# Nine more 512-column chunks of a two-block layer as seven block products, with a weight ring of three slots

## The reference, cut to what matters

```python
h = rms_norm(x, g_norm);  proj = h @ w_in             # q_a k_a v_a q_i ... q_m z_m gate_logits
branch = einsum('nbsw,nwd->nbsd', ys, w_branch)
merged = einsum('bsnd,nbsd->bsd', sigmoid(gate_logits), branch)
x = x + merged @ w_out                                 # wout0, wout1
...
h = _rmsnorm(x, norm_mix);  h @ w_in_2                 # dq dk (diff. attention), gv gg gqk gr (GLA), dv
kv = _rmsnorm(mem_2, norm_mem) @ w_ckv                 # ckv0 .. ckv3
```

## Time and profile before

| | before |
|---|---|
| median of the 3 runs (lowest, highest) | 1147.48 us (1147.24, 1147.68) |
| the profiled execution: its time, its span | 1148.03 us, 1146.3 us |
| PE busy | 943.7 us, 82% |
| DVE, ACT, POOL busy | 341.6, 175.3, 102.6 us |
| DMA, share of 16 engines over the span | 63.9%, 253 GB/s |
| mean granted clock of PE | 0.925 of full speed (2.4 GHz) |

### The profile page before, as it was taken

How to read it: one execution, slowest core, us unless ns; L and a number is a source line. 1 busy time by engine, 2 the same in 40 slices (tenths; PEclk the granted TensorE clock), 3 DMA queues, 4 the chain that set the end, 5 groups by cost and what they waited for, 6 DMA issues and landing times.

```text
span 1146.3 us, 11508 instructions
## 1 busy us (share of the span) xinstructions
PE 943.7 (82%) x4732; PEld 531.3 (46%) x4732; DVE 341.6 (30%) x879; ACT 175.3 (15%) x380; POOL 102.6 (9%) x121
## 2 busy tenths in 40 slices
PE   7999999899999999999999999565655566565736
PEld 3555485679999464455544555221221212131312
DVE  3217933764232221535545424010000101010101
ACT  2114232431000012212312211000000000000000
POOL 2013110145443010100000000000000000000000
PEclk9999999999999999999999999887787878697979
DMA  9546232224445264432209458999999999999996
GB/s 327 177 154 219 85 137 74 74 75 147 148 148 185 75 220 146 147 144 77 74 1 342 177 219 340 430 428 427 428 429 428 428 428 427 428 427 428 429 420 240
DMA packets 64020, 290.33 MB, mean 253 GB/s; under 512 B 8983, under 2 KB 11870, under 8 KB 52190
## 3 DMA queue, kind: packets, MB, share of 16 engines
q1 hardware_dynamic: 63966, 289.57, 63.9%
HBM read 288.51 MB, written 1.05 MB: 253 GB/s over the span
## 4 chain that ended last, share of the span: by engine, by line
PE 62%; DMA 28%; DVE 5%; SPq 2%; ACT 2%; issue 1%; ACTq 0%; DVEq 0%
PE ACC L500 24%; PE ACC L515 8%; PE AUX L1033 7%; PE ACC L643 6%; DMA ring<-in_w_e_down_dram 5%; DMA ring<-in_w_e_gate_dram 5%; PE ACC L539 4%; PE AUX L1063 3%; DMA BIG<-in_w_e_up_dram 3%; DMA PJ<-in_w_e_up_dram 3%; DMA SQE<-in_w_e_up_dram 3%; DMA PJ<-in_w_e_down_dram 3%; DMA BIG<-in_w_e_gate_dram 2%; PE ACC L925 2%; DMA SQE<-in_w_e_gate_dram 2%; PE AUX L550 2%
## 5 line engine op out<-in xcount | busy, mean ns | idle before, releaser
L1033 PE MATMUL AUX<-ring,R 128*32 128x512 f32 x416 | 115.4, 718 | 53.6 <-DMA BIG<-in_w_e_up_dram 20.2
L500 PE MATMUL ACC<-ring,BIG 128*128 128x512 f32 (+2 forms) x384 | 159.1, 573 | 0.2 <-ACT BIG L1513 0.2
L500 PE MATMUL ACC<-ring,R 128*128 128x512 f32 (+1 forms) x296 | 129.2, 590 | 2.8 <-DVE R L1677 2.1
L500 PEld LDWEIGHTS ACC<-ring,BIG 128*128 128x128 f32 x384 | 72.5, 190 | 81.6 <-issue 73.6
L515 PE MATMUL ACC<-BIG,ring 128*128 128x256 f32 (+1 forms) x464 | 107.3, 385 | 0.0
L515 PEld LDWEIGHTS ACC<-BIG,ring 128*128 128x128 f32 (+1 forms) x464 | 85.2, 188 | 16.1 <-issue 4.1
L500 PEld LDWEIGHTS ACC<-ring,R 128*128 128x128 f32 x296 | 55.8, 192 | 65.4 <-issue 64.2
L1033 PE MATMUL AUX<-R 128*32 128x512 f32 x112 | 62.7, 723 | 24.7 <-DMA ring<-in_w_e_gate_dram 14.6
L1033 PE MATMUL AUX<-BIG,R 128*32 128x512 f32 x192 | 55.6, 745 | 29.0 <-DMA PJ<-in_w_e_up_dram 22.3
L2187 DVE SCALAR_TENSOR_TENSOR R<-R,AUX 128x512 f32<-128x512 f32 x8 | 5.5, 687 | 235.9 <-ACT R L1608 235.9
L1033 PEld LDWEIGHTS AUX<-ring,R 128*32 128x32 f32 x416 | 28.3, 129 | 93.4 <-issue 93.4
(11 more groups left out here) (311 smaller groups left out, 1287.6 us busy)
## 6 DMA issues: line engine op xcount, KB each, us to landing
ring<-in_w_in_dram SPq DMA_DIRECT2D x20, 2048.0 KB, 7.9
ring<-in_w_e_gate_dram SPq DMA_DIRECT2D x14, 2048.0 KB, 27.2
ring<-in_w_e_up_dram SPq DMA_DIRECT2D x12, 2048.0 KB, 30.8
ring<-in_w_e_down_dram SPq DMA_DIRECT2D x10, 2048.0 KB, 30.1
PJ<-in_w_e_down_dram SPq DMA_DIRECT2D x8, 2048.0 KB, 31.7
BIG<-in_w_e_up_dram SPq DMA_DIRECT2D x8, 2048.0 KB, 32.4
PJ<-in_w_e_gate_dram SPq DMA_DIRECT2D x6, 2048.0 KB, 27.3
BIG<-in_w_e_down_dram SPq DMA_DIRECT2D x6, 2048.0 KB, 26.4
```

The lines of the kernel that those rows point to most:

```text
L500: mm = nc.tensor.matmul(bank[:, t * 512:t * 512 + width], lhs[:, i, t * P:(t + 1) * P], w[:, i, a:a + width], start=(i == 0), stop=(i == k ...
L1033: mm = nc.tensor.matmul(bank[r, :], M_xt[:, k, r], w[e][:, k, :], start=(k == 0), stop=(k == KD - 1))
```

## The change

Besides the six gates, nine chunks become seven block products: qm, wout0, wout1, ckv0, dq, dk, gv, ckv1 and gg. They take a second form of `project_blocks`: rows stationary, weights moving, 28 matmuls of 256 columns. The gates keep their own form (`turned=True`). The fourth slot of the ring is set aside: it holds S_a, S_b (first half) and T_x (second half), and the ring has three slots until ckv2; wo1 and wco1 are then loaded into the fourth. ckv3 is loaded before wo0. The fourth weight sum is now written over w12, may start after m1 and m2, and S_b no longer waits for the whole chunk before. POOL makes weight sums for all 15 chunks; the row sums for merged, mem_2 and x1 are made by DVE (`row_sums`, four instructions each). DVE sums the products of each chunk (`combine`, eight instructions), and so it, not ACT, frees the PSUM banks of these chunks. ckv0 and ckv1 are scaled by ACT afterwards in SBUF, gg's tanh is read from SBUF, and the sum into x is made from a temporary (`TMP`).

```diff
-        T_x = R2[:, :].rearrange("p (i k q) -> p i k q", i=4, k=4)
+        block_chunks = ["qm"] + gate_chunks + ["wout0", "wout1", "ckv0", "dq", "dk", "gv", "ckv1", "gg"]
+        WS = slots[RING - 1]
+        S_a, S_b = (WS[:, 1024 * i:1024 + 1024 * i].rearrange("p (k n) -> p k n", k=4) for i in range(2))
+        T_x, T_mem2 = (t.rearrange("p (i k q) -> p i k q", i=4, k=4) for t in (WS[:, 2048:4096], R5[:, 2048:4096]))
...
+        c = chunk_at["ckv2"]
+        slot_no = [i % (RING - 1) for i in range(c + 3)] + [RING - 1] + [i % (RING - 1) for i in range(c, c + 3)] + [RING - 1]
...
+            def project_blocks(name, src, T, sums, base=0, after=None, turned=False):
+                w11, w12, w21, w22 = (w[:, 4 * j:4 * j + 4, 256 * i:256 * i + 256] for i in range(2) for j in range(2))
+                x = quarters(src)
+                products = [(w11, x[0][0], 0, 0), (w12, x[1][0], 0, 0), (S_a, T[:, 0], 1, 1), (S_b, T[:, 1], 3, 2),
+                            (w21, T[:, 2], 0, 3), (w22, T[:, 3], 0, 4), (w12, x[1][1], 4, 0)]
...
+                                mm = nc.tensor.matmul(bank, right[:, k, :], left[:, k, :], start=(k == 0), stop=(k == 3))
...
-            project("wout0", R1T, ready=merged_half)
-            project("wout1", R1T)
+            pe.wait_ge(merged_ready, 1)
+            project_blocks("wout0", R1T, T_x, merged_sums, after=lambda done: pe.wait_ge(merged_ready, 2) if done == 4 else None)
+            project_blocks("wout1", R1T, T_x, merged_sums)
...
-            project("dq", XT3)
-            project("dk", XT3)
-            project("gv", XT3)
-            project("ckv1", R2T)
+            project_blocks("dq", XT3, T_x, x1_sums)
+            project_blocks("dk", XT3, T_x, x1_sums)
+            project_blocks("gv", XT3, T_x, x1_sums)
+            project_blocks("ckv1", R2T, T_mem2, mem2_sums)
...
+            def weight_sums(name):
...
                 if c:
                     pool.wait_ge(block_products, 3 * c - 1)
                 add(S_a, w21, w22, ALU.add, w_sums, 4 * c + 1)
                 add(w21, w11, w21, ALU.subtract, w_sums, 4 * c + 2)
-                if c:
-                    wait_full(pool, (gate_chunks[c - 1], "high"))
                 add(S_b, S_a, w11, ALU.subtract, w_sums, 4 * c + 3)
-                pool.wait_ge(block_products, 3 * c + 2)
-                add(S_b, w12, S_b, ALU.subtract, w_sums, 4 * c + 4)
...
+                pool.wait_ge(block_products, 3 * c + 1)
+                add(w12, w12, S_b, ALU.subtract, w_sums, 4 * c + 4)
...
+            row_sums(T_x, quarters(kt(R1[:, :], KD)), merged_sums)
             drain_rows("mem2", R2T, GC_MEM2)
+            wait_drained(dve, ("mem2", 1, 1))
+            row_sums(T_mem2, quarters(R2T), mem2_sums)
             dve.wait_ge(rows_squared, 4)
             rsqrt(2, SMALL[:, 64:66], SMALL[:, 78:80]).then_inc(mem2_scaled, 1)
...
+            for h in range(2):
+                combine(f"wout{h}", by_rows(TMP))
+                part = X3[:, :, h * 512:(h + 1) * 512]
+                v.scalar_tensor_tensor(out=part, in0=TMP, scalar=0.25, in1=part, op0=ALU.mult, op1=ALU.add).then_inc(x_added, 1)
...
+            combine("dq", by_rows(DQ))
             dve.wait_ge(decay_e, 1)
...
+            combine("dk", by_rows(DK))
+
+            def apply_d():
+                combine("gv", by_rows(GV), range(2))
+                scale_heads(hv(DQ[:, 0, :], 8), 0, 8)
+                scale_heads(hv(DK[:, 0, :], 8), 16, 8)
+                combine("gv", by_rows(GV), range(2, 4))
```

More of the change, by code:

```diff
@@ L638, in project_blocks @@
                     bank = (low if m < 4 else high)[:, 256 * (m % 4):256 * (m % 4) + 256]
[L639 to L645 removed]
+                    if w_sum:
+                        pe.wait_ge(w_sums, 4 * c + w_sum)
+                    if x_sum:
+                        pe.wait_ge(sums, base + x_sum)
+                    for j in range(2 if turned else 1):
+                        for k in range(4):
+                            if turned:
+                                mm = nc.tensor.matmul(bank[:, j * P:(j + 1) * P], left[:, k, j * P:(j + 1) * P], right[:, k, :],
+                                                      start=(k == 0), stop=(k == 3))
+                            else:
+                                mm = nc.tensor.matmul(bank, right[:, k, :], left[:, k, :], start=(k == 0), stop=(k == 3))
+                            n += 1
+                            last = k == 3 and (j == 1 or not turned)
+                            if m == 6 and last:
                                 mm.then_inc(high_full, 1)
[L647 removed]
+                            elif m in (1, 3, 5) and last:
                                 mm.then_inc(block_products, 1)
@@ L774, in end_m @@
                     attend("M", 4 + (done - 6) // 12, 5 + (done - 6) // 12)
-            project_blocks("gate00", start_m)
-            project_blocks("gate01", end_m)
+            project_blocks("gate00", XT3, T_x, x0_sums, after=start_m, turned=True)
+            project_blocks("gate01", XT3, T_x, x0_sums, after=end_m, turned=True)
             wait_drained(pe, ("O", first_unit["A"] + 7))
@@ L1317, in _ @@
             g.tensor_tensor(KE, kt(GK, 2), kt(EE, 2), ALU.mult).then_inc(gla_products, 1)
+            for name in ("gv", "ckv1", "gg"):
+                weight_sums(name)
             for t in range(TT):
@@ L1507, in drain_mem2, with scale_mem2 @@
                 last.then_inc(free_sem(key), 1)
-            drain_mem2("ckv0", R1v, 0)
+            def scale_mem2(key, T3, c):
+                wait_drained(act, key)
+                for t in range(TT):
+                    part = T3[:, t, c:c + 512]
+                    last = a_.activation(part, part, ACT.Copy, scale=SMALL[:, 78 + t:79 + t])
+                link(last)
+            scale_mem2("ckv0", R1v, 0)
             drain("gr", [(GRT[:, :], lambda b: b[0:16, 0:S])])
```

231 lines of the change are left out of this document (118 added, 113 removed).

## The result

The changed kernel takes 1154.78 us (median of 4 runs, 1154.24 to 1155.85) against 1147.36 us for the kernel before, measured beside it (4 runs, 1147.14 to 1147.68): ratio 1.007, 95% interval 1.0057 to 1.0083. It is slower, as was forecast: by 7.4 us, where the forecast had 4.6. The profiled execution took 1154.90 us, its span is 1153.1; the one before took 1148.03, span 1146.3.

A forecast was written before the change was run, and what follows sets the result against it. PE was taken to bound the kernel up to about 700 us, the expert weights' DMA stream from 716 us. Costs of 23.4 us less 18.8 saved gave +4.6 on 1147.48, so 1152.1 us, own range 1148 to 1156, overall range 1134 to 1157.

The forecast's parts named there:

- A chunk of 12.1 us, 1.66 saved: Each of nine chunks on PE, as 56 instructions of 256 columns, takes 12.1 us; 14.9 us saved for nine.
- Around qm, 3.0 of at most 4.2 us: At qm, earlier sums and no ACT drain remove PE's waits of 1.17, 1.59 and 1.00 us; 3.0 us saved, bounds 0 to 4.2.
- Three waits: 7.3, 6.8 and 7.8 us: Before wout1, dk and ckv1, PE waits this long for the low bank, as POOL's sums hold DVE's two-SBUF-input instructions.
- the second rival's case: Before dk, POOL does not hold the decay chain's scans: wait 3.3 us, not 6.8; 1148.6 us; chance 0.18, shared with one wait halved or absent.
- gr 0.8, gv's fourth product 0.7: Smaller PE waits: gr 0.8 us for ckv0's bank, gv's fourth product 0.7 us for S_b.
- The ring of three, nothing: Weight loads with three slots: 7.9 us to land, wanted 19 us after issue, 11 us of slack, so no cost.
- The wait of 0.86 us at wcq1: PE's wait at 611 us for wcq1 goes, since its slot is free earlier; 0.86 us saved.
- One for one to the end: What PE gains or loses before the cross attention ends moves the whole expert-weight stream equally; expert gates start about 4.6 us later.
- the first rival: Waits on POOL do not bind: cost 1.5 + 0.7 us, saving 18.8, giving 1130.9 us; waits mostly absent had chance 0.24.
- The ring starves nobody: Judges the rival that loads taking 19 us instead of 7.9 make PE wait: 1153 to 1160 us, chance 0.04.
- The change reaches the end: Judges the rival that the expert stream hides the change: 1147.5 us, chance 0.04.

The follow-up runs named there:

- pe_fill_half: Changed kernel plus useless matrix products on PE behind wout0 (17), dq (15) and gv (17), to keep it busy through the three waits: 1149.90 us.
- order_three: Changed kernel with DVE's work reordered at three places and POOL's at one, around the combines of wout0, dq, gv and dk; nothing left out: 1144.86 us.
- no_pool_sums: Changed kernel with POOL's first three weight sums for wout1, dk, gv and ckv1 replaced by tiny memsets, so those chunks use stale sums: 1129.01 us.
- order_five: order_four with gg and the turn of KE ahead of the turned heads on PE, and the QLZ copies behind the norm chain: 1137.72 us.
- order_four: order_three with mem_2's rsqrt behind both wout combines, combine(gv) split between the padded copies, combine(ckv1) inside and around the norm chain: 1143.07 us.

## Why the prediction came out as it did

**The direction was right, and so was the mechanism of the waits; what the clock adds behind a wait was missing.** That the time still fell between 1148 and 1156 us is in part luck: with the clock's 6.7 us alone the forecast's 1152.1 would have become 1158.8. Too small a saving (3.6 us, most of it around qm) and a last stretch that was 2.3 us shorter took that back. The terms, as the trace has them:

- *A chunk of 12.1 us, 1.66 saved.* gg took 12.09, against 13.74 before. Right.
- *Around qm, 3.0 of at most 4.2 us.* Too small. Between the starts of qm and gate00 the change saves 7.4 us, of which 1.65 is qm itself: 5.75 for the waits, over the forecast's upper bound. The step that failed took PE's waits alone as the price. The window of the kernel before shows the rest (stretch, length, busy us of PE, PEld, DVE, ACT, POOL, clock, DMA share, GB/s):

```profile
204.00:241.40 37.40, 31.92 (x184) 24.59 (x185) 29.31 (x63) 15.43 (x49) 12.88 (x7) 0.95 0.13 52
```

and the same work in the changed kernel:

```profile
202.00:234.00 32.00, 29.74 (x182) 23.16 (x181) 23.43 (x63) 15.15 (x49) 0.82 (x1) 1.00 0.18 65
```

  With the same products PE is busy 2.2 us less, at a clock of 1.00 in place of 0.95, and idle 3.2 less (5.48 against 2.26). In the kernel before the clock fell behind the waits of 1.17 and 1.59 us (windows of PE alone):

```profile
216.00:218.00 2.00, 0.99 (x4) 0.75 0.00 0
218.00:220.00 2.00, 2.00 (x6) 0.50 0.02 4
```

  The waits were sized about right; the clock behind them was not in the sum.
- *Three waits: 7.3, 6.8 and 7.8 us.* They were 8.02, 6.96 and 7.75. The instructions were the right ones: `L1967` and `L1969` of mem_2 and `L1673` at over 2 us. The scans are held, 7.88 us for eight, which takes the second rival's case away; the two subtractions behind them were not (0.69 each), since POOL's last sum had ended. Not foreseen: that plain TENSOR_SCALAR instructions with a single SBUF input (`L2029`, `L1661`, `L1662`) are held as well. At each of the three places one of them met a POOL sum and took 2.3 to 2.5 us. The bank was free little off the count all the same, from the start of the chunk: 20.3 us for 19.4 at wout1, 19.3 for 18.9 at dk, 19.8 for 20.6 at ckv1.
- *The clock behind the waits: not in the sum at all.* 6.7 us by the chunks. This is the step that was mis-sized: a wait was priced at its length. In `pe_fill_half` the filling took 4.9 us off the time.
- *gr 0.8, gv's fourth product 0.7.* 0.42 and none.
- *The ring of three, nothing.* Right: behind the load of `mem` at the very start (6.0 us, 5.9 before) PE waits for no DMA before 600 us. The wait of 0.86 us at wcq1 is gone, as forecast. The +0.5 us at the start is not the ring's: mk took 15.67 us before and 16.07 after, but among the experiments, all with the ring of three, 15.67 (`order_three`) as well as 16.55 (`no_pool_sums`). It differs between traces with the same ring.
- *One for one to the end.* Within what the traces can tell. From the expert gates' start to the end of the span it was 446.6 us before and 444.3 after, so 9.1 us at 699.75 became 6.8 at the end. But in the experiments this stretch took 443.9 (`no_pool_sums`) to 447.5 us (`order_five`), so it isn't shown that the change gives these 2.3 us back. The first expert load is issued 3.9 us later than before (622.29 against 618.39), the one for the ring at 681.34 9.1 us later, so the stream's first part moved less than PE did. Which part sets the end was not tried and stays open.

The ledger from qm's start to gg's: eight chunks at 1.65 to 1.70 saved, 13.4 us; 5.75 around qm; 0.7 between gate00 and wout0 (130.5 us against 131.2), for which the forecast had no term; 23.5 of waits and 6.7 of clock lost. That is +10.3 us, where the trace has 318.80 against 307.49, +11.3. Of the missing 1.0 some 0.8 is an estimate from PE's rows: the idle time in brackets is counted from the modelled end of the row before (377.24 for wout0), 0.16 us behind the 12.09 of a chunk, at five waits. gg's 1.65 and wcq1's 0.86 off and 0.5 of the start on give +9.3 at the expert gates (+9.1 measured). The forecast for that point was +4.6: it lacked the 6.7 of the clock, the 0.5 of the start and this 1.0, and counted 2.75 too little saved around qm, 0.7 in the gates and 0.1 in the columns. Put right, that makes 9.3; 0.2 stays unassigned.

**The rivals.** The waits bind. Without twelve of POOL's sums, most of those beside the three waits, the time is 1129.0 us, and the first rival gave 1130.9: its price was near, and its condition was not met. The scans do not pass. The ring starves nobody. The change reaches the end.

## What to carry to other kernels

When a change gives one engine more instructions, look at what stands queued ahead of the one that releases somebody, and price that queue with the neighbour's work beside it, not with its old durations; then move the releasing instruction ahead, part by part, and follow the work that slips behind it, for it can be held there again. Price a stall of TensorE as its length plus what the clock loses behind it: here 1.8 to 2.5 us on top of each 7 to 8. Do not count on a short stall being free of it, as the two waits of 2.21 us show. And a saving that comes off in one place and is lost in another is worth splitting: one of the nine chunks alone, with what goes with it, gave 5.2 us (1146.6 to 1141.4), and all nine gave 15 once the order was better (1146.5 to 1131.6).

## What the runs showed that had not been expected

- Eight scans (`ones` and `SQE`) took 1.57 us with POOL silent and 7.88 beside its sums, one waiting per sum. The Trainium skill (SBUF — State Buffer, Who interferes with whom) gives the lock for two SBUF inputs and for the two-port modes, which `tensor_scalar` can enter; the rows of `L2029` (2.51 us beside a sum, 0.43 without) and of the scans agree with both parts, the second of which the forecast had not used.
- In a chain of small dependent steps about two were done per POOL sum, one held and one that slipped through behind it (`L1672` 2.23, `L1673` 0.19, `L1675` held again). Twelve steps that take 0.18 to 0.19 us each alone took 10.8 us (471.60 to 482.43).
- What a short wait of PE does to the clock differed. One of 2.65 us (`order_four`) left it at 1.00 and one of 3.80 (`order_five`) cost 1.8 us more. One of 2.21 left it at 1.00 in `order_four`, and in `order_five` the clock fell to 0.50 behind it and that cost some 1.6 (7.0 us from the turns of x1 to gr, against 5.4 in `order_four`). In the kernel before it fell to 0.50 around qm's heads, behind waits of 1.17 and 1.59 us with little between them.
- Products with no use, set into a stall, made the kernel 0.4% faster than the changed one (1149.90 against 1154.78).
